# A chunked RWKV-7 recurrence on one core: the chunk step cut into four dense pieces, two inverse levels with two heads side by side, and a chunk's loads split by the buffer they overwrite

## The reference, cut to what matters

```python
def step(state, inp):
    r_t, w_t, k_t, v_t, a_t, b_t = inp
    sa = jnp.einsum('bhij,bhj->bhi', state, a_t)
    state = (state * w_t[:, :, None, :] + sa[..., None] * b_t[:, :, None, :]
             + v_t[..., None] * k_t[:, :, None, :])
    return state, jnp.einsum('bhij,bhj->bhi', state, r_t)
_, y = lax.scan(step, jnp.zeros((Bsz, H, N, N), jnp.float32), xs)
```

## Time and profile before

| what | value |
|---|---|
| median of 3 runs | 2167.01 us (2163.85 to 2167.51) |
| the profiled execution | 2165.27 us, span of its instructions 2163.5 us |
| mean granted clock of TensorE | 0.987 of full |
| TensorE busy | 2077.2 us, 96% of the span |
| VectorE, ScalarE, GpSimd busy | 1264.9, 928.6, 504.6 us |
| the chunk stage on TensorE | first start 240.11 us, last start 475.8 us |

### The profile page before, as it was taken

The page is one execution under the profiler, slowest core; times in us unless marked ns, Lnnn a source line. Parts: engine busy times, 40 slices in busy tenths (PEclk is TensorE's granted clock), DMA queues, the critical chain, the costliest instruction groups (busy, mean ns, idle before and its releaser), DMA issues. The chain is left out here.

```text
span 2163.5 us, 36481 instructions
## 1 busy us (share of the span) xinstructions
PE 2077.2 (96%) x14738; PEld 1680.8 (78%) x14739; DVE 1264.9 (58%) x1270; ACT 928.6 (43%) x1067; POOL 504.6 (23%) x357
## 2 busy tenths in 40 slices
PE   8999999999999999999999999999799999999996
PEld 6777777766787787888887788787588888888882
DVE  4767422215320565346568814355798888888885
ACT  4662122224101464022245412002587777777763
POOL 3232311102350101334323332200122222222200
PEclk9999999999999999999999999999899999999998
DMA  4445624434441543421143432231699999999985
GB/s 150 138 119 190 179 80 116 118 108 143 176 149 37 139 92 111 141 99 42 48 125 117 144 120 86 99 139 58 218 411 391 386 385 384 388 382 387 381 337 238
DMA packets 138136, 408.48 MB, mean 189 GB/s; under 512 B 38736, under 2 KB 60112, under 8 KB 112800
## 3 DMA queue, kind: packets, MB, share of 16 engines
q1 hardware_dynamic: 123104, 367.40, 48.6%
q10 hardware_dynamic: 5552, 22.02, 2.7%
q0 software_dynamic: 9360, 17.32, 2.1%
HBM read 353.53 MB, written 69.93 MB: 196 GB/s over the span
## 5 line engine op out<-in xcount | busy, mean ns | idle before, releaser
L3467 DVE TENSOR_TENSOR ex_sb_low<-landed,high 128x2048 fp32r<-128x2048 f32 x192 | 431.1, 2287 | 61.3 <-ACT high L3396 57.8
L3396 ACT CAST high<-landed 128x2048 fp32r<-128x2048 f32 x186 | 346.1, 1910 | 39.2 <-PE ex_ps_u L169 35.6
L3281 POOL DMA_INDIRECT y_rows<-ex_sb_y,slot_row x32 | 32.3, 1010 | 438.8 <-ACT ex_sb_y L3411 420.8
L167 PE MATMUL ex_ps_g<-high,ex_sb_xt 128*128 128x512 f32 x260 | 104.7, 403 | 2.4 <-DVE ex_sb_xt L3461 2.4
L169 PE MATMUL ex_ps_g<-high,ex_sb_xt 128*128 128x512 f32 x260 | 102.3, 393 | 0.0
L168 PE MATMUL ex_ps_g<-ex_sb_low,ex_sb_xt 128*128 128x512 f32 x260 | 102.1, 393 | 0.0
L167 PE MATMUL ex_ps_u<-high,ex_sb_xt 128*128 128x512 f32 x260 | 101.3, 390 | 0.5 <-DVE ex_sb_low L3467 0.5
L169 PE MATMUL ex_ps_u<-high,ex_sb_xt 128*128 128x512 f32 x260 | 101.2, 389 | 0.0
L168 PE MATMUL ex_ps_u<-ex_sb_low,ex_sb_xt 128*128 128x512 f32 x260 | 101.2, 389 | 0.0
L1116 DVE TENSOR_TENSOR rc_sb_ab<-rc_ps_m,mats 128x512 f32<-128x512 f32 x32 | 20.6, 686 | 133.6 <-PE rc_ps_m L984 133.6
L169 PE MATMUL ex_ps_y<-high,ex_sb_ht 128*128 128x512 f32 x248 | 96.7, 390 | 0.0
(11 more groups left out here) (663 smaller groups left out, 5552.7 us busy)
## 6 DMA issues: line engine op xcount, KB each, us to landing
landed<-exp_up SPq DMA_DIRECT2D x64, 1024.0 KB, 8.5
landed<-exp_gate SPq DMA_DIRECT2D x64, 1024.0 KB, 7.7
landed<-exp_down SPq DMA_DIRECT2D x62, 1024.0 KB, 8.8
chunk_ch<-slab SPq DMA_DIRECT2D x4, 2048.0 KB, 7.5
merged_d<-room SPq DMA_DIRECT2D x16, 512.0 KB, 2.9
landed<-ssm_c SPq DMA_DIRECT2D x16, 512.0 KB, 4.7
cb_sb_y<-y_rows SPq DMA_DIRECT2D x16, 512.0 KB, 9.7
si_sb_w<-w_tiles SPq DMA_DIRECT2D x14, 512.0 KB, 3.6
```

The costliest lines, as they stand in the source:

```text
L167: nc.tensor.matmul(out, lhs[0], rhs[0], start=start, stop=False)
L3281: pool.indirect_dma_start(k.y_rows, bass.IndirectOffsetOnAxis(ap=k.slot_row[:, e:e + 1], axis=0), y[e % 2][:, :], None, bounds_check=2 * T ...
L3396: nc.scalar.copy(part_half(high[part], h), part_half(k.landed[part], h)).then_inc(high_ready[part], 1)
L3467: nc.vector.tensor_tensor(part_half(low[part], half), part_half(k.landed[part], half), part_half(high[part], half), ALU.subtract).then_inc ...
```

## The change

On TensorE, `products` is called by group (n, m), and one step of the middle now reads: level 3 of the chunk before, products, through 0, products, **fill 0-4**, products, through 1, level 0, products, through 2, **fill 4-8**, level 1, through 3, **fill 8-12**, level 2, **fill 12-16**. Level 3 has moved across the step's boundary: it belongs to the back now. The fill stands in four segments of four groups instead of six of two or three. In the first step it stands in the gaps between the groups of products and levels (3, 3, 2, 2, 3, 3). The eighth step now has 12 groups and the last has 4, the last with level 3 ahead of through 0.

In levels 2 and 3, even heads write one half of the partitions of `ps_l` and odd heads the other, in turn; before, all eight heads wrote the same half. The copies that follow are split: ScalarE takes the even heads, VectorE the odd ones. That adds two VectorE instructions a chunk (64x256 each) and shortens two of ScalarE's. VectorE's copy for level 3 comes ahead of the masks of its step, the one for level 2 behind the update of the state.

On SyncE the one wait for two signals becomes three waits: `bk` after level 1 of chunk c-2 (`x5_done`), two `tok` pieces and the blocks after the state's sums (`s_done`), `ar` and the first `tok` piece after the output (`y_done`).

```diff
+        def own_half(n, h):
+            at = (n + h) % 2
+            return slice(at * HD, at * HD + HD)
...
-                        sp.wait_ge(s_done, c - 1)
-                        sp.wait_ge(y_done, c - 1)
+                        wait_apart(sp, x5_done, c - 1, stood)
...
                         for h in range(RH):
-                            last = mm(wide(0)[HD:P, h, :], ab[b][0:HD, h, HD:P], x[b][0:HD, h, 0:HD], start=True, stop=True)
+                            last = mm(wide(0)[own_half(1, h), h, :], ab[b][0:HD, h, HD:P], x[b][0:HD, h, 0:HD],
+                                      start=True, stop=True)
                         last.then_inc(z6_done, 1)
                     else:
-                        wait_apart(pe, z6_copied, c + 1, stood)
+                        wait_apart(pe, z6_copied, 2 * c + 2, stood)
...
+                        level(back, 3)
+                        products(front, 0, 0)
+                        through(back, 0)
+                        products(front, 0, 1)
+                        fill(c + 1, 0, 4)
+                        products(front, 1, 0)
+                        through(back, 1)
+                        level(front, 0)
+                        products(front, 1, 1)
+                        through(back, 2)
+                        fill(c + 1, 4, 8)
...
+                        dve.wait_ge(x6_done, bc + 1)
+                        v.tensor_copy(xt[bb][0:HD, 1:RH:2, HD:P], wide(1)[own_half(0, 1), 1:RH:2]).then_inc(x6_copied, 1)
...
+                        dve.wait_ge(z6_done, c + 1)
+                        v.tensor_copy(z6[HD:P, 1:RH:2, :], wide(0)[own_half(1, 1), 1:RH:2]).then_inc(z6_copied, 1)
...
-                        copy(z6[HD:P, :, :], wide(0)[HD:P]).then_inc(z6_copied, 1)
+                        copy(z6[HD:P, 0:RH:2, :], wide(0)[own_half(1, 0), 0:RH:2]).then_inc(z6_copied, 1)
...
-                        copy(xt[b][0:HD, :, HD:P], wide(1)[0:HD]).then_inc(x6_copied, 1)
+                        copy(xt[b][0:HD, 0:RH:2, HD:P], wide(1)[own_half(0, 0), 0:RH:2]).then_inc(x6_copied, 1)
```

More of the change, by code:

```diff
@@ L947, in step @@
                                          ).then_inc(x_in[b], 16)
+                    if not early:
+                        wait_apart(sp, y_done, c - 1, stood)
+                    for n in range(2):
+                        q = slice(n * HD, n * HD + HD)
+                        sp.dma_start(ar[b][q, :, n, :], src[q, :, 0:2 * P]).then_inc(loaded[b], 16)
+                    load_tok(0)
                     for j in range(0 if early else 1, 2):
@@ L971, in fill, with products @@
                             last.then_inc(used, 1)
-                def products(front, back, n):
+                def products(front, n, m):
                     c, b, early = front
-                    if n == 0:
+                    if n == 0 and m == 0:
                         pe.wait_ge(loaded[b], (c - b) * 48 + 96)
-                    for t in range(RT):
-                        if t == 2:
-                            fill(c + 1, 3 * n, 3 * n + 3)
+                    for t in (2 * m, 2 * m + 1):
                         for o in range(2):
                             q = slice(o * HD, (o + 1) * HD)
-                            if t % 2 == 0 and not (n == 0 and t == 0 and isinstance(c, int) and c == 0):
-                                pe.wait_ge(masked[o], 4 * c + 2 * n + t // 2)
+                            if t % 2 == 0 and not (n == 0 and t == 0 and c == 0):
+                                pe.wait_ge(masked[o], 4 * c + 2 * n + m)
                             last = mm(ps_m[o][:, (t % 2) * 2 * P:(t % 2 + 1) * 2 * P], bk[b][q, t, n, :], ar[b][q, t, o, :],
@@ L1070, in step @@
                 def step(front, back):
[L1071 to L1089, removed]
+                    if front is None:
+                        level(back, 3)
+                        through(back, 0)
+                        fill(NT, 12, 14)
+                        through(back, 1)
+                        fill(NT, 14, 16)
+                        through(back, 2)
+                        through(back, 3)
+                        return
@@ new lines, in step @@
+                    c = front[0]
+                    if back is None:
+                        products(front, 0, 0)
+                        fill(c + 1, 0, 3)
+                        products(front, 0, 1)
+                        fill(c + 1, 3, 6)
+                        products(front, 1, 0)
+                        level(front, 0)
+                        fill(c + 1, 6, 8)
+                        products(front, 1, 1)
+                    else:
+                        level(back, 3)
+                        products(front, 0, 0)
+                        through(back, 0)
+                        products(front, 0, 1)
+                        fill(c + 1, 0, 4)
+                        products(front, 1, 0)
+                        through(back, 1)
+                        level(front, 0)
+                        products(front, 1, 1)
+                        through(back, 2)
+                        fill(c + 1, 4, 8)
@@ new lines, in step @@
+                    if back is None:
+                        fill(c + 1, 8, 10)
+                        level(front, 1)
+                        fill(c + 1, 10, 13)
+                        level(front, 2)
+                        fill(c + 1, 13, 16)
+                    else:
+                        level(front, 1)
+                        through(back, 3)
+                        if last_pass(c):
+                            fill(c + 1, 8, 10)
+                            level(front, 2)
+                            fill(c + 1, 10, 12)
+                        else:
+                            fill(c + 1, 8, 12)
+                            level(front, 2)
+                            fill(c + 1, 12, 16)
@@ L1106, in step @@
                 def step(front, back):
+                    if back is not None:
+                        bc, bb = back[0], back[1]
+                        dve.wait_ge(x6_done, bc + 1)
+                        v.tensor_copy(xt[bb][0:HD, 1:RH:2, HD:P], wide(1)[own_half(0, 1), 1:RH:2]).then_inc(x6_copied, 1)
                     if front is not None:
@@ L1118, in step @@
                     if back is not None:
-                        bc, bb = back[0], back[1]
                         dve.wait_ge(s_done, bc + 1)
@@ L1125, in step @@
                            k.decays[:, :, bass.ds(bc, 1)].to_broadcast([P, RT, HD]), ALU.mult).then_inc(s_scaled, 1)
+                    if front is not None:
+                        dve.wait_ge(z6_done, c + 1)
+                        v.tensor_copy(z6[HD:P, 1:RH:2, :], wide(0)[own_half(1, 1), 1:RH:2]).then_inc(z6_copied, 1)
                 steps(dve, step)
@@ L1189, in step @@
                     if front is not None:
-                        for n in range(3):
+                        for n in range(2):
                             level(front, n)
@@ L1196, in step @@
                     if front is not None:
-                        level(front, 3)
+                        level(front, 2)
                 act.wait_ge(k.gate_out, 16)
```

18 lines of the change are left out of this document (10 added, 8 removed).

## The result

The changed kernel takes 2150.93 us (median of 6 runs, 2147.77 to 2154.39), the kernel before 2167.48 in the same series. The ratio is 0.9924, 95% interval 0.9911 to 0.9937: 16.5 us less (13.7 to 19.3 by the interval), where 15.5 were forecast. Its profiled execution took 2151.73 us with a span of 2149.9, 13.6 less than before's span.

What follows compares the result with a forecast made beforehand. TensorE, busy 232.79 of 240 us, bounds the stage. Gains of 6.9 + 2.2 + 3.6 + 0.9 + 0.8 + 0.3 = 14.7 us give 2150.6 (profile) or 2152.3 (median); forecast 2151.5 us, 8-in-10 range 2145 to 2160.

Steps and rivals of the forecast that it cites:

- Levels 2 and 3: On TensorE, heads in turn bring each level from 1.07 to 0.65 us, gaining 6.9 us over 8 chunks.
- Fewer borders: TensorE's stage has 132 pieces instead of 143, each with a fixed part of 0.20 us: 2.2 us gained.
- The mask wait: Products stop waiting for VectorE's masks: 0.40 us in seven steps and 0.78 in the first, 3.6 us gained.
- The loads: TensorE's waits for `ar` go, 0.9 us gained; loads land 6.6 us after the output, first product at 7.2.
- The eighth and the last step: Level 3's copy wait goes in the eighth, 0.8 us; half the last through 0's instruction gap goes, 0.3 us.
- The first step: `ar` lands behind the blocks, first product up to 1 us later, but fill waits for GpSimd anyway: price 0.
- The sum: All terms of the chunk stage together: 14.7 us gained.
- pairs don't overlap: Rival: the order changes but levels 2 and 3 stay at 1.07 us; 7.8 us gained, 2158.5 us; chance 0.08.
- the loads come too late: Rival: loads miss TensorE's 7.2 us window, clock halves, about 2174 us; chance 0.04 for a loss, 0.07 mildly late.
- instructions run short: Rival: dense pieces leave TensorE's queue short, one gap in each of 7 steps, 3.6 us, 2155 us; chance 0.09.
- a stage behind changed its own length: Sign of being wrong: stages after the chunk stage, expected to move as a whole, change length; no size given.

Runs made afterwards that it cites:

- e6: The changed kernel with the first two fill segments of a middle step each cut in two around a dense piece; ratio to before 0.9930.
- e2: The changed kernel with levels 2 and 3 and their copies as before, new order and new loads kept; ratio to before 0.9945.
- e4: The kernel before with only the new split of the loads; ratio to before 0.9996.
- e5: The kernel before with the levels' heads in turn and the new split of the loads, pieces in old order; ratio to before 0.9949.
- e1: The kernel before with only levels 2 and 3 with heads in turn and their copies shared, old order and loads; ratio to before 0.9984.
- e3: The changed kernel with the old loads, one wait for both signals ahead of all of them; ratio to before 1.0044.
- e8: The changed kernel with two groups of fill moved from the last step into the eighth, behind level 2; ratio to before 0.9925.
- e7: The changed kernel with the first half tile of fill weights loaded first, and `ar` and `tok` ahead of the blocks in the first two steps; ratio to before 0.9903.
- e9: The kernel of e7 with the last step's through 0 cut in its middle by two groups of fill; 2145.14 us, ratio to before 0.9902.

## Why the prediction was right, step by step

*Levels 2 and 3.* Right: 0.61 against a forecast of 0.65, 16 x 0.46 = 7.4 us instead of 6.9. Two places side by side gave 0.41 / 16 = 0.026 us a matmul, close to through 2's 0.028. The Trainium skill ("TensorE: Matmul & The Clock Gate", Part 3, The mechanism) has weight loads overlap only across row groups. These pairs share their 64 rows, and the trace doesn't agree: with 0.61 instead of 1.07 they run at nearly twice the rate.

*Fewer borders.* Right, a little small: 0.24 us a border (e6) instead of 0.20; for 11 borders that makes an estimated 2.6 us.

*The mask wait.* Right: the fourth group takes 1.07, and the first step's 0.78 is gone, 3.6 us. Order against old order in the same setting (e2 and e4) is 27.14 - 26.28 = 0.86 a step, which is 0.40 and two borders (0.48).

*The loads.* The step of the prediction that was mis-stated. I put them in as a term of 0.9 us, the waits that the profile named. The waits did go, and the window was as thin and as sufficient as computed (7.16 us). But through 0 had lost 1.5 us in five steps, not 0.9, and all of it went with the split alone (e4). Above all the term is not one that adds: each gain on the way from the output to the first product shortens the time for the loads. The split is worth 2.1 us of stage in the old order (e4 against before; 0.8 of it is the first step, with its scatter), 6.1 with the shorter levels (e5 against e1), 24.4 with the new order too (e3 against the changed kernel). The forecast was saved by having both parts in it.

*The eighth and the last step.* The wait of 0.76 for a copy went, and with like work the eighth step is 2.46 shorter, as the terms give. In the last step the missing instructions cost 0.5 us more, where 0.3 less were forecast. I had read the gap as a queue emptied by a wait; in ten traces it ends 2.35 to 2.65 us after the start of a packet of instructions, and it is longer where the levels are shorter (e8).

*The first step.* Cost 0 forecast. The first product waited 1.83 us for `tok`, not up to 1. The fill's weights came 15.8 us after the stage's start instead of 14.4, but also 15.0 to 15.4 in e1 to e6, with either order of loads: that part is scatter of the transfers. With like work the step is 0.97 shorter, where two levels, a mask wait and one more border give 1.46, so the cost was 0.5 us. The idle time itself could be removed (e7).

*The sum.* 14.7 forecast, 14.95 in the stage. By terms it was levels 7.4, borders 2.6, masks 3.6, loads 1.5 and eighth step 0.8, less 0.5 in the last and 0.5 in the first step: 14.9. Three terms were 1.5 us too small together (levels, borders, loads) and two 1.3 too good (first and last step), and that the sum is off by 0.2 only is luck. So is part of the agreement of the times: the profiled executions differ by 13.6, the medians by 16.5, and the interval is 13.7 to 19.3. Of the rivals, "pairs don't overlap" and "the loads come too late" fell; "instructions run short" showed once, in the last step. One sign that the prediction named for being wrong did show: a stage behind changed its own length. The merge took 1.2 us more, by the clock, which the prediction had left out.

## What to carry to other kernels

Where one engine is busy from end to end, price its pieces from start to start, split off the fixed part of each border, and a reordering can be forecast to a few tenths of a microsecond a step. A transfer hidden behind such a row has no price of its own, only a window: recompute the window after every gain inside it, and release each buffer's load by its own last reader before shortening the row. A gap that stays at one instruction count while work moves around it belongs to the instruction stream: look in the DMA view for the packet that ends it. Here slow instructions between that packet's start and the gap helped, more work ahead did not. And compare steps with like work, at like clock: a piece that has crossed a step's border, or a few matmuls at 1.2 GHz, look like a gain or a loss of the change.

## What the runs showed of the hardware

The same idle time can cost the clock or not. In the merge stage TensorE waits 2.1 to 2.2 us for VectorE in both kernels. Stretches of 7.5 us with this wait in the middle, before:

```profile
512.50:520.00 7.50, 5.08 (x21) 3.53 (x20) 4.82 (x4) 3.44 (x3) 0.00 (x0) 1.00 0.08 34
```

After:

```profile
497.10:504.60 7.50, 5.30 (x16) 3.58 (x15) 4.71 (x4) 3.44 (x3) 0.00 (x0) 0.80 0.10 40
```

PEclk is 1.00 and 0.80: the changed kernel ran part of this at 1.2 GHz. The twelve matmuls behind the wait took 1.35 us longer; the stage as a whole gave back 1.2. Idle times there of 1.73 to 2.24 us kept the full clock in before, e1 and e3, the three kernels with the old loads; 2.06 to 2.30 us lost it in the eight with the new loads. No run tells whether that is more than chance.

At the chunk stage's start the contrast is sharper. All eleven kernels run the same program up to there and wait 2.06 or 2.07 us at the barrier. Seven kept the full clock behind it; in e4, e5, e6 and e9 some eight matmuls of fill ran at 1.2 GHz, a granted clock of 0.87 over the stage's first 13 us, which costs up to 1.6 us. So the length of an idle time doesn't decide, and one trace of each kernel can differ by this much with nothing changed; what does decide was not settled.
